# A spectrum moved into the transforms' block, and two norms moved tile by tile into the second projection's block

## The reference, cut to what matters

```python
# first block, mixer (u_f, k_f: transforms of the signal and of the filter)
k = k / jnp.sum(jnp.abs(k), axis=0, keepdims=True)
k_f = jnp.fft.rfft(k, n=2 * L, axis=0)
u_f = jnp.fft.rfft(u, n=2 * L, axis=1)
z = irfft(u_f * k_f)[:, :L] + z * f_bias ;  y_hyena = x0 * z
# end of the first block: residual plus two weighted expert rows per token
x = rmsnorm(x + hierarchical_moe(...), final_g)
# start of the second block
h = rms_norm(x, norm_mix_pre)
q, k, v, u, gates = split(h @ w_in)
```

## Time and profile before

| | us |
|---|---|
| median of 3 runs | 2657.0 (2656.66 to 2662.24) |
| the profiled execution's own time | 2663.09 |
| its span, first to last instruction | 2661.3 |
| PE busy in it | 2415.0 (91%) |
| DVE, ACT, POOL busy | 1586.4, 1064.5, 443.6 |

### The profile page before, as it was taken

One profiled execution on the slowest core, in us unless ns is written; L12 is line 12 of the kernel. 1 busy time (PEld: TensorE's weight loads), 2 busy tenths in 40 slices (PEclk: granted clock), 3 DMA queues, 4 the chain that ended last, 5 costly groups with the idle time before them and its releaser, 6 DMA issues. The chain is left out here.

```text
span 2661.3 us, 28228 instructions
## 1 busy us (share of the span) xinstructions
PE 2415.0 (91%) x11032; PEld 1836.7 (69%) x11032; DVE 1586.4 (60%) x1697; ACT 1064.5 (40%) x1270; POOL 443.6 (17%) x295
## 2 busy tenths in 40 slices
PE   7999967948999999963998999997969999998998
PEld 5775544846666666642877768886758888876877
DVE  5552575348999999957111652222489998873343
ACT  4220203226777777744112751112344344433332
POOL 3110301001222222313200210000032333310000
PEclk9999987969999999985999999999989999998999
DMA  4120222259999999965111001113202222225443
GB/s 156 48 64 0 64 97 94 80 217 332 387 379 389 381 376 379 380 227 213 47 41 64 2 29 48 47 48 115 102 32 88 95 80 87 80 76 210 130 154 135
DMA packets 191845, 397.25 MB, mean 149 GB/s; under 512 B 16023, under 2 KB 119575, under 8 KB 175337
## 3 DMA queue, kind: packets, MB, share of 16 engines
q1 hardware_dynamic: 182504, 378.76, 39.9%
q0 software_dynamic: 9216, 16.80, 2.0%
HBM read 357.75 MB, written 47.18 MB: 152 GB/s over the span
## 5 line engine op out<-in xcount | busy, mean ns | idle before, releaser
L1547 DVE TENSOR_TENSOR expert_rest<-expert_raw,expert_high 128x2048 fp32r<-128x2048 f32 x124 | 281.0, 2289 | 41.9 <-ACT expert_high L1541 30.5
L141 PE MATMUL up_ps<-blocks_high,up_operand_high 128*128 128x512 f32 x616 | 241.6, 392 | 14.3 <-DVE up_operand_rest L3245 14.3
L1541 ACT ACTIVATE expert_high<-expert_raw 128x2048 fp32r<-128x2048 f32 x124 | 237.2, 1913 | 23.2 <-PE expert_up_ps L143 8.1
L143 PE MATMUL up_ps<-blocks_high,up_operand_rest 128*128 128x512 f32 x616 | 241.3, 392 | 0.0
L1547 DVE TENSOR_TENSOR expert_rest<-res,expert_high 128x2048 fp32r<-128x2048 f32 x68 | 154.5, 2290 | 21.0 <-ACT expert_high L1541 20.5
L1927 POOL DMA_INDIRECT expert_rows<-y_rows,out_ids x32 | 90.6, 2831 | 415.2 <-DVE y_rows L1887 415.2
L141 PE MATMUL down_ps<-w_down_high,prod_high 128*128 128x512 f32 x352 | 139.3, 396 | 16.2 <-DVE w_down_rest L181 16.2
L141 PEld LDWEIGHTS up_ps<-blocks_high,up_operand_high 128*128 128x128 f32 x616 | 116.7, 189 | 39.7 <-DVE up_operand_rest L3245 15.4
L3245 DVE TENSOR_TENSOR up_operand_rest<-res,up_operand_high 128x512 fp32r<-128x512 f32 x154 | 142.3, 935 | 0.2 <-ACT up_operand_high L3200 0.2
L142 PE MATMUL down_ps<-w_down_rest,prod_high 128*128 128x512 f32 x352 | 138.9, 395 | 0.0
L142 PE MATMUL up_ps<-plain_blocks_rest,up_operand_high 128*128 128x512 f32 x352 | 138.7, 394 | 0.0
(11 more groups left out here) (413 smaller groups left out, 6029.2 us busy)
## 6 DMA issues: line engine op xcount, KB each, us to landing
expert_raw<-in_w_gate_dram SPq DMA_DIRECT2D x42, 1024.0 KB, 13.8
expert_raw<-in_w_down_dram SPq DMA_DIRECT2D x42, 1024.0 KB, 17.0
expert_raw<-in_w_up_dram SPq DMA_DIRECT2D x40, 1024.0 KB, 16.1
res<-in_w_in_dram SPq DMA_DIRECT2D x48, 512.0 KB, 4.2
res<-in_w_up_dram SPq DMA_DIRECT2D x24, 1024.0 KB, 18.1
res<-in_w_down_dram SPq DMA_DIRECT2D x22, 1024.0 KB, 14.7
res<-in_w_gate_dram SPq DMA_DIRECT2D x22, 1024.0 KB, 18.6
res<-in_w_up_dram SPq DMA_DIRECT2D x88, 256.0 KB, 4.0
```

The source lines that it names most:

```text
L141: nc.tensor.matmul(out, w_high, x_high, start=start, stop=False)
L143: return nc.tensor.matmul(out, w_rest, x_high, start=False, stop=stop)
L1541: self.nc.scalar.activation(self.high_part[:, n % SPLIT_SLOTS, :], self.raw[n % RAW_SLOTS], ACT.Copy) \
L1547: self.nc.vector.tensor_tensor(self.rest_part[:, s, :], self.raw[n % RAW_SLOTS], self.high_part[:, s, :].bitcast(F32), ALU.subtract).then_ ...
```

## The change

Two parts. **The spectrum** is no block any more: its PE, ACT and DVE work stands inside `transform_mixes`, after the 64 record transform and ahead of the channel transforms. The size matmuls move into `project_first` after job 13. POOL's folding waits for `U_done`, as its place now is that of the odd part. z is scaled by `bias_size` (size times `f_bias`), PE adds it in PSUM with eight identity matmuls, and one DVE instruction per quarter makes the output; POOL gates nothing. **The norms** are no blocks any more: `combine` and `norm_to_T` are gone, and `project_second` does a loop over the tiles in which both norms, the transposes and hT's two parts follow each other tile by tile. Gamma is made a row and multiplied into `scaled`; DVE makes `hT_rest` straight from PSUM. The ring has four slots; the first two raw tiles lie in `poolT` for their first use. From tile 4 on, PE makes the first token half of the first four jobs between the transposes, and the second halves after the last tile. The residual is stored tile by tile, and the bias rows are copied behind the sixth weight tile. The section's end comes after this block instead of ahead of norm3.

```diff
@@ project_first @@
+                if c == SIZE_AFTER:
+                    pe.wait_ge(filt.size_step, 2 * 2 * JT + 1)
+                    for n in range(HT):
+                        last = nc.tensor.matmul(filter_ps[:, 0, n:n + 1], filt.size[:, n * P:(n + 1) * P], m.ones[:, 0:1],
+                                                start=True, stop=True)
+                    last.then_inc(filt.size_mm, 1)
...
+                        nc.vector.reciprocal(m.inv_size[:], filter_ps[:, 0, 0:HT])
+                        nc.vector.tensor_tensor(m.bias_size[:], filter_ps[:, 0, 0:HT], m.params[:, at:at + n], ALU.mult)
@@ transform_mixes, tensor @@
+            pe.wait_ge(filt.lags_done, 2 * JT)
+            pe.wait_ge(split_done, 3)
+            even(0)
+            pe.wait_ge(split_done, 4)
+            pe.wait_ge(neg_done, 2)
+            odd(0)
+            pe.wait_ge(spec_even_done, 1)
+            even(1)
+            pe.wait_ge(spec_done, 1)
+            odd(1)
             pe.wait_ge(pair_in, 16)
-            pe.wait_ge(split_done, 3)
+            pe.wait_ge(spec_even_done, 2)
             channel_transform(0)
-            pe.wait_ge(split_done, 4)
+            channel_transform(1)
+            pe.wait_ge(spec_done, 2)
...
             pe.wait_ge(four_kept, 2 * HT + 1)
+            pe.wait_ge(bias_done, HT)
+            for c in range(HT):
+                for par in range(2):
+                    nc.tensor.matmul(ps[:, 2 * c + par, :].rearrange("p (s i) -> p s i", s=2), m.ident[:], of_parity(m.zT, c, par),
+                                     start=True, stop=False)
@@ gpsimd @@
+            pool.wait_ge(U_done, 1)
...
-            for n in range(2 * HT):
-                if gated_by_pool(n):
...
@@ vector @@
+            last.then_inc(U_done, 1)
+            dve.wait_ge(U_done, 1)
+            for trig in range(2):
...
+                dve.wait_ge(spec_mm, 2 * trig + 2)
+                nc.vector.tensor_tensor(m.K[:, trig, 0, :, :], spec_even, ps[:, 4:8, :], ALU.add)
+                nc.vector.tensor_tensor(m.K[:, trig, 1, :, :], spec_even, ps[:, 4:8, :], ALU.subtract).then_inc(spec_done, 1)
...
+                        out=x0, in0=ps[:, 2 * c + par, :].rearrange("p (s i) -> p s i", s=2), scalar=m.inv_size[:, c:c + 1],
+                        in1=x0, op0=ALU.mult, op1=ALU.mult)
@@ project_second, sync @@
+            for n in range(2):
+                ring.load(sp, n, 0, ring_source(n), first=True)
...
+            sp.wait_ge(m.y_out[0], (count + EXPERTS // 2) * 16)
+            expert_rows(0)
+            sp.dma_start(final_row, A["final_g"].to_broadcast([P, D])).then_inc(final_in, 16)
+            expert_rows(1)
+            for n in range(2, EARLY):
+                ring.load(sp, n, 0, ring_source(n), first=True)
+                expert_rows(n)
+            for t in range(TT):
+                if t + BUF < TT:
+                    sp.wait_ge(summed, t + 1)
+                    expert_rows(t + BUF)
+                sp.wait_ge(normed, t + 1)
+                sp.dma_start(m.res_dram[t * P:(t + 1) * P, :], m.res[:, t, :]).then_inc(kept[t] if t < 2 else others_kept, 16)
...
@@ tensor @@
+            for t in range(TT):
+                pe.wait_ge(scaled_done, t + 1)
+                if t >= 2:
+                    pe.wait_ge(out_done, t - 1)
+                for k in range(KT):
+                    last = nc.tensor.transpose(turn_ps(t)[:, k // 4, k % 4, :], scaled[:, t % 2, k * P:(k + 1) * P], m.ident[:])
+                last.then_inc(turned, 1)
+                if t >= TT - EARLY:
+                    j = t - (TT - EARLY)
+                    if j == 0:
+                        pe.wait_ge(out_done, TT // 2)
+                        pe.wait_ge(row_done, 1)
+                    ring.arrived(pe, j, 0)
+                    half_product(j, 0)
+            pe.wait_ge(out_done, TT)
+            for j in range(EARLY):
+                half_product(j, 1).then_inc(ring.used[j], 1)
...
+                pe.wait_ge(job_out, {EARLY: 2, EARLY + 1: EARLY}.get(j, j - 3))
@@ scalar @@
+            for t in range(TT + 2):
+                if 2 <= t < EARLY:
+                    ring.high(act, t, 0, first=True)
+                if t >= 2:
+                    act.wait_ge(turned, t - 1)
+                    nc.scalar.activation(tile_of(hT[0], t - 2), turn_ps(t - 2), ACT.Copy).then_inc(high_done, 1)
+                if 1 <= t <= TT:
+                    square(1, t - 1)
+                if t < TT:
+                    if t:
+                        act.wait_ge(squared[1], t)
+                    square(0, t)
@@ vector @@
+            for t in range(TT + 2):
+                if 1 <= t <= TT:
+                    final_norm(t - 1)
+                if t < TT:
+                    put_together(t)
+                if 1 <= t <= TT:
+                    next_norm(t - 1)
+                if t >= 2:
+                    leave(t - 2)
+                if 2 <= t < EARLY:
+                    ring.rest(dve, t, 0)
+            dve.wait_ge(others_kept, 16 * (TT - 2))
@@ second_block @@
+                section.close()
+                section.enter_context(m.section(nc))
```

More of the change, by code:

```diff
@@ L166, in __init__, with place @@
         self.used = [m.sem(f"{name}_used{s}") for s in range(slots)]
+    def place(self, s, use):
+        return (self.first_raw if isinstance(use, int) and use == 0 else self.raw)[s]
     def load(self, engine, s, use, source, first=False):
@@ L2297, in project_second, with turn_ps, bank, tile_of @@
         NW = len(tiles) + KT // 2
+        assert tiles[:EARLY] == jobs[:EARLY]
+        def turn_ps(t):
+            return ps[:, 2 + t % 2, :, :].rearrange("p q (k c) -> p q k c", c=P)
+        def bank(j, half):
+            return ps[:, 2 * half + j // 2, j % 2, :] if j < EARLY else ps[:, j % 4, half, :]
+        def tile_of(part, t):
+            return part[:, :, t * P:(t + 1) * P].rearrange("p (q k) c -> p q k c", q=2)
         def ring_source(n):
@@ L2341, in _ @@
                 for half in range(2):
-                    cols = slice(half * BANK, (half + 1) * BANK)
-                    for k in range(KT):
-                        last = product(nc, ps[:, j % 4, half, :], ring.parts(n % S, k),
-                                       (hT[0][:, k, cols], hT[1][:, k, cols]), start=(k == 0), stop=(k == KT - 1))
+                    last = half_product(j, half)
                 last.then_inc(ring.used[n % S], 1)
@@ L2388, in _ @@
                     out = (m.qT if kind == "q" else m.kT)[:, c, :]
-                if out is not None:
+                if j < EARLY:
+                    for half in range(2):
+                        last = nc.scalar.activation(out[:, half * BANK:(half + 1) * BANK], bank(j, half), ACT.Copy,
+                                                    scale=HEAD ** -0.5 if kind == "q" else 1.0)
+                    last.then_inc(job_out, 1)
+                elif out is not None:
                     nc.scalar.activation(out.rearrange("p (h c) -> p h c", h=2), ps[:, j % 4, :, :], ACT.Copy,
@@ L2425, in _, with put_together @@
         def _(dve):
+            def put_together(t):
+                dve.wait_ge(y_in[t % BUF], 32 * (t // BUF + 1))
+                for slot in range(2):
+                    if slot:
+                        dve.wait_ge(half_summed, t + 1)
+                    nc.vector.scalar_tensor_tensor(out=m.res[:, t, :], in0=y[:, t % BUF, slot, :],
+                                                   scalar=m.pair_w[:, slot, t:t + 1], in1=m.res[:, t, :],
+                                                   op0=ALU.mult, op1=ALU.add).then_inc((half_summed, summed)[slot], 1)
```

557 lines of the change are left out of this document (191 added, 366 removed).

## The result

The changed kernel takes **2637.5 us** (median of 4, 2636.3 to 2639.4), the kernel before 2656.8 beside it (2656.0 to 2662.2): a ratio of 0.9919, interval 0.9907 to 0.9932. Faster, by 19 us by the medians (21 by the ratio), where 35 were forecast. The two profiled executions lie 23.7 apart (2663.1 and 2639.4); the 4.4 between the two numbers is where each stood in its own spread.

What follows compares the result with a forecast made beforehand. PE, busy over 90% of the span, was taken as the bound, with gains where it waits: spectrum -18.0 and norms -17.3, together -35.3, from the median 2657.0 to 2621.7; likeliest case 2612 to 2631, stated range 2609 to 2640.

Steps and rivals of the forecast that it cites:

- the 15 us wait: Mixer: PE's wait of 15.17 us ahead of the fourth back tile group, ending at 372.75, was to disappear.
- rival A: Second projection: PE's clock stays at 1.2 GHz through the four early halves, costing 17.2 us: 2639; chance 0.10.
- Spectrum, up to the Fourier transform: Mixer: size matmuls add 0.95 us, K's last operation ends at 306.9, the Fourier transform starts at 311.3.
- Their moving operand takes every fourth float ... I take +1.7, nearer PE's own row: Mixer, eight identity matmuls: 6.9 us plus 1.7 for the strided operand, between +0.5 and +4.4.
- The back transform and its tables: Mixer: fourth tile lands at 358.5, before its need at 360.6, so PE runs through; the other 80 records take 18.6 us.
- Rival B: Mixer: the spectrum part pays half, through a DVE or tile wait or full strided cost (+4.4): 2631; chance 0.11.
- Between 0 and 8.8 for two tiles; I take 3.4: Second place: two weight tiles issued ahead of the expert rows delay the rows by 3.4 us, to 1192.5.
- Tile loop, S + 40.6: Second place: PE's first half product comes 40.6 us after the rows' start S (1192.5), at 1233.1; DVE takes 6.7 a tile.
- rivals C and D: Second place: weight tiles or `leave` too late to hide early halves, 2643, chance 0.06; ACT and DVE alternating waits, 2658, 0.03.
- The clock: Second projection: PE starts at 1.2 GHz, so the first 14 products are slow, 6.1 us, then 0.227 us each.
- Rival E: Second projection: the clock does not return before v; with all 562 products slow +118 us, 2740; chance 0.03.
- Boundary: Section's end, moved behind the second projection: the path pays 0.75 us there.

## Why the forecast was right, and where it failed

The sign and the range held, the size did not: the forecast's own 2612 to 2631 is missed (its ends add up to 2613 and 2630). In the profiled executions 35.3 were forecast and 23.7 came. Of the signs that it named, the 15 us wait is gone and K is in time; the identity matmuls (14.6) lie above its 11.3, the next block starts 3 us later than said, the first half product came at 1225.6 and not near 1215, and the projection's end 26 earlier and not 35, mostly from the two misses below. The range held because it reached up to rival A's 2639; A did not come, and two other misses used its room, which is luck. By steps:

- **Spectrum, up to the Fourier transform:** right. Size matmuls +1.1 (0.95). K's last operation ends at 306.5 (306.9 forecast), and the Fourier transform starts at 310.3, 1.0 before the sum's 311.3, which did not yet hold the size matmuls; with them it is 1.9.
- **"Their moving operand takes every fourth float ... I take +1.7, nearer PE's own row":** the failed step. It is +7.7 (14.64 - 6.9), above even the upper end of 4.4; with sorted data the same products take 7.1. Of this 6.0 too little, 1.9 was won back ahead of the Fourier transform and the rest in small parts behind. The bounds came from two steps of another kind: DVE on the same quarters, and PE with every second float. The Trainium skill's rule (SBUF — State Buffer, Door 1: The DMA port swizzle) was the one that pointed the right way, since four floats fill one 16-byte line: a step of two floats has two hits in each line, a step of four has one. I had cited it and then gone by a row on its other side.
- **The back transform and its tables:** right. 29.2 us without a wait, 29.7 forecast. Part 1 came to -14.8, and not -18.0. Rival B had half of it: the operand costs fully, and more than its +4.4, but no table group was late.
- **A step that the sum took for granted, at a price of nothing:** that 14.8 us gained ahead of the experts arrive behind them. 8.9 were lost there in the changed kernel (+8.9 in the table). I had read the experts as PE's stage. They are PE's and the DMA queues' at once: 376 GB/s and a DMA share of 1.01 beside a PE without a gap, so that a per cent or two less in the loads ends as waits. Of the 8.9, 5.7 are lost by the kernel before as well once its slots stand at the same place, and padding brings 5 to 7 us of the time back: that part was not the work of either edit, but of its 16 bytes of allocation. What the other 3.2 are is open. This was no rival either, and it is the largest part of the 11.6 between forecast and result. Without it the forecast's size would have been nearly right, the strided operand's miss partly made up by part 2, and that much is luck.
- **"Between 0 and 8.8 for two tiles; I take 3.4":** right; 2.9 in the trace and by the run with the rows first.
- **Tile loop, S + 40.6:** 38.8. DVE bounds it as forecast, and rivals C and D are out: `leave` is in time, and a tile takes 5.6 us without `leave` (the first two), then 6.4 to 7.9.
- **The clock:** five slow products where 14 were counted. Rival A would have had all early halves slow; their products stand 0.23 apart in the trace, and the run with late halves shows what they are worth, 19.5 to 21.7. Rival E is out with it.
- **Boundary:** +1.05 (5.41 instead of 4.36 ahead of the band attention); 0.75 forecast. From the last copy to the band attention part 2 gave 19.9, forecast 17.3.
- **Behind:** nothing was forecast; +1.4 came: +2.1 in the gates' products, +2.5 where the granted clock was lower, -2.8 in the last projection and some tenths beside. Why, no run shows.

The sum of the differences is 3.2 (part 1) + 9.5 (to the last expert's copy, 0.6 of it ahead of the experts) - 2.6 (part 2) + 1.4 (behind) = 11.5, of the 11.6 to be explained.

## What to carry to other kernels

Before a gain is carried through a later stage, look whether that stage has slack at all: one with both PE and DMA at 100% hands a gain on only if its loads keep their rate, and a new small tile ahead of the load buffers can change that by itself. So compare a change with a kernel before whose buffers stand at the same place, and not only with the plain one. A step of four floats in a matmul's moving operand cost as much as the matmul again, at full clock; sorting once on an idle engine pays, if that engine does not share its time with a chain that is nearly critical. After taking a wait away, look in the queue that carried it for what else stands behind the same semaphore.

## What the runs showed of the hardware beyond what was expected

- A 128x512 fp32 matmul product with a step of four floats in the moving operand: a record every 0.90 us, against 0.43 on contiguous data, both at full granted clock (1.00). At 0.50 the strided ones kept their 0.90, where contiguous ones went to 0.85.
- 32 or 64 bytes of padding cost the kernel before some 6 us by the ratios (5 and 8 by the medians); 32 to 96 gave the changed one 5 to 7. Weight loads of 1 MB landed in 12.4 to 14.8 us (median) with their slots at 0 modulo 256, in 16.7 or more elsewhere.
- DVE's operations on SBUF took 4.13 instead of 2.36 us a pair while POOL worked on SBUF too. The Trainium skill (SBUF — State Buffer, Who interferes with whom) has that a DVE instruction with two SBUF inputs contends with a GpSimd instruction that reads SBUF, and these rows agree. It also has that one of the two holds the shared pair for its whole instruction; that these rows don't show. Of the first pair one operation took 3.00 and the other 1.21, and the one of 3.00 ended at 313.95, while POOL's first instruction (309.78 to 314.61) still ran; POOL's took 4.2 to 5.3 each, and 3.8 alone.
